# Three projections of the matrix memories moved into the gated recurrence's loop

## The reference

```
hg_q, hg_i, hg_g, hg_f_fwd, hg_f_bwd, ml_q, ml_k, ml_v, ml_o, ml_gates = split(h_all @ w_in)
# first half: gated recurrence, 4 heads of 128, in both directions
log_f = log(lb + (1 - lb) * sigmoid(f_pre)); k_in = (1 - lb) * sigmoid(-f_pre)
hg_o = both_directions(S_t = diag(f_t) S_{t-1} + k_t v_t^T ; o_t = S_t^T q_t)
hg_out = head_rmsnorm(hg_o, hg_norm_w) * silu(hg_g)
# second half: matrix memories, 4 heads, in both directions
qk = silu(short_conv([ml_q, ml_k], conv_w, conv_b))  # 3x3 over the 8 x 64 latent grid, 3 taps over the context
ml_h = both_directions(mlstm(q, k, ml_v, i_gate, log_sigmoid(f_gate)))
ml_out = sigmoid(ml_o) * head_rmsnorm(ml_h, ml_norm_w)
lat_out = concat(hg_out, ml_out)[latent] @ w_out
```

## Time and profile before

| | |
|---|---|
| median of 3 runs | 3689.83 us (3689.51 to 3694.19) |
| the profiled execution | 3686.75 us |
| its span | 3683.8 us |
| PE busy | 3358.1 us, 91% of the span |
| DVE busy | 1669.8 us, 45% |
| ACT busy | 1164.0 us, 32% |
| POOL busy | 976.3 us, 27% |
| mean granted TensorE clock | 0.938 |

### The profile page before, as it was taken

One profiled execution on the slowest core, in us unless ns is written; L12 is line 12 of the kernel. 1 busy time (PEld: TensorE's weight loads), 2 busy tenths in 40 slices (PEclk: granted clock), 3 DMA queues, 4 the chain that ended last, 5 costly groups with the idle time before them and its releaser, 6 DMA issues. The chain is left out here.

```text
span 3683.8 us, 42189 instructions
## 1 busy us (share of the span) xinstructions
PE 3358.1 (91%) x17058; PEld 2672.1 (73%) x17058; DVE 1669.8 (45%) x2625; ACT 1164.0 (32%) x1874; POOL 976.3 (27%) x414
## 2 busy tenths in 40 slices
PE   4999989989999799999997777979999888889998
PEld 3887767867888688888786665358887664568887
DVE  5995576554331323345401886532211576631211
ACT  2232364334442421121322113433222324543322
POOL 0001312433444122323332002024444221024443
PEclk8999999989999899999999778979999888899999
DMA  4232324442233122334321001012233110013332
GB/s 177 93 100 89 134 89 158 154 160 69 98 95 95 65 87 94 126 133 139 107 69 40 1 2 51 1 57 91 96 110 96 46 52 26 1 58 96 96 94 86
DMA packets 91197, 315.98 MB, mean 86 GB/s; under 512 B 10742, under 2 KB 12534, under 8 KB 90234
## 3 DMA queue, kind: packets, MB, share of 16 engines
q1 hardware_dynamic: 88060, 303.69, 25.2%
q10 hardware_dynamic: 2944, 9.60, 0.7%
HBM read 311.16 MB, written 2.10 MB: 85 GB/s over the span
## 5 line engine op out<-in xcount | busy, mean ns | idle before, releaser
L245 POOL TENSOR_TENSOR terms<-streams,terms 128x1024 fp32r<-128x1024 f32 (+2 forms) x410 | 976.1, 2381 | 2685.0 <-ACT terms L233 2685.0
L455 PE MATMUL bank<-terms,terms 128*128 128x512 f32 (+2 forms) x4016 | 1508.7, 376 | 46.8 <-DVE terms L699 17.3
L456 PE MATMUL bank<-terms,terms 128*128 128x512 f32 (+2 forms) x4016 | 1499.7, 373 | 0.0
L457 PE MATMUL bank<-terms,terms 128*128 128x512 f32 (+2 forms) x4016 | 1497.5, 373 | 0.0
L233 ACT ACTIVATE terms<-streams 128x1024 fp32r<-128x1024 f32 (+1 forms) x462 | 475.9, 1030 | 1831.7 <-PE bank L457 1653.6
L455 PEld LDWEIGHTS bank<-terms,terms 128*128 128x128 f32 x4016 | 764.9, 190 | 202.1 <-issue 48.7
L457 PEld LDWEIGHTS bank<-terms,terms 128*128 128x128 f32 x4016 | 765.4, 191 | 132.1
L456 PEld LDWEIGHTS bank<-terms,terms 128*128 128x128 f32 x4016 | 766.4, 191 | 126.1
L1620 DVE TENSOR_TENSOR stage<-stage,bank 128x256 f32<-128x256 f32 (+1 forms) x88 | 54.7, 622 | 596.4 <-ACT stage L1610 596.4
L1063 DVE SCALAR_TENSOR_TENSOR arena<-arena,vec 128x512 f32<-128x512 f32 x240 | 162.4, 744 | 0.2
L1603 DVE TENSOR_TENSOR terms<-stage,terms 128x512 fp32r<-128x512 f32 (+1 forms) x66 | 116.5, 1769 | 0.0
(11 more groups left out here) (320 smaller groups left out, 2984.8 us busy)
## 6 DMA issues: line engine op xcount, KB each, us to landing
streams<-in_ffn_w SPq DMA_DIRECT2D x104, 512.0 KB, 3.5
streams<-in_w_mod SPq DMA_DIRECT2D x72, 512.0 KB, 3.5
streams<-in_w_up SPq DMA_DIRECT2D x44, 512.0 KB, 3.5
streams<-in_w_gu SPq DMA_DIRECT2D x44, 512.0 KB, 3.5
streams<-in_w_ada SPq DMA_DIRECT2D x32, 512.0 KB, 3.5
streams<-in_w_down SPq DMA_DIRECT2D x32, 512.0 KB, 3.5
streams<-in_w_v SPq DMA_DIRECT2D x24, 512.0 KB, 3.8
streams<-in_ffn_w SPq DMA_DIRECT2D x24, 384.0 KB, 3.3
```

The lines of the kernel that those rows point to most:

```text
L245: gp.tensor_tensor(self.low(m), self.raw(n), self.high(m), ALU.subtract).then_inc(self.low_made.sem, 1)
L455: pe.matmul(out, high[:, at], x_high, start=kk == start, stop=False)
L456: pe.matmul(out, high[:, at], x_low, start=False, stop=False)
L457: mm = pe.matmul(out, low[:, at], x_high, start=False, stop=kk == kts - 1)
```

## The change

`MemoryInputs` takes the projections of keys, queries and output gates out of `memory_inputs` and gives one of their eight tiles to each of the recurrence's eight units, in the order keys, queries, output gates. Behind the scores of each level stands one k tile (three matmuls; for the keys two k tiles of one of the two token ranges, the context behind levels 0 to 3 and the latent behind 4 to 7). All use bank 3, and the scores turn through banks 0 to 2. SP fetches and GpSimd makes a low half in each unit; ScalarE evicts the tile and casts a high half after placing the last level's scores. The low halves beside `w_mo` are no longer VectorE's. The stage behind keeps head norms, gates, taps and the gate chain. Taps read unpadded tiles: a tap works on the part of the grid for which its neighbour exists, the centre tap comes first, and each tap waits for the one before it. The gate chain's scans stand behind the taps on VectorE.

```diff
+    dense("w_mk")
+    dense("w_mq")
+    dense("w_mo")
     dense("w_gates")
-    dense("w_mq")
-    dense("w_mk")
-    dense("w_mo")
...
-    k.vector_lows.update(range(k.plan["w_mo"][0][0][0], k.plan["w_out2"][0][0][0]))
...
+    def some(self, pe, n, c, a, b, told=None):
...
+        if a == 0:
+            if uses:
+                pe.wait_ge(k.bank_free[bank].sem, uses)
+            pe.wait_ge(k.low_made.sem, m + 1)
...
+        for kk in range(a, b):
+            at = slice(kk * cols, (kk + 1) * cols)
+            x_high, x_low = self.src(kk, c)
+            pe.matmul(out, high[:, at], x_high, start=kk == 0, stop=False)
+            pe.matmul(out, high[:, at], x_low, start=False, stop=False)
+            mm = pe.matmul(out, low[:, at], x_high, start=False, stop=kk == kts - 1)
...
+    def bank(n, lev):
+        return B[(8 * n + lev) % 3]
...
+        @block.sync
+        def _(sp):
+            for n in range(len(units)):
+                inputs.fetch(sp, n)
+
+        @block.gpsimd
+        def _(gp):
+            for n in range(len(units)):
+                inputs.low(gp, n)
...
             for n in range(len(units)):
+                inputs.keep_context(act, n, tiled)
                 if n + 1 < len(units):
...
                 place(n, levels - 1)
                 place(n, levels)
+                inputs.keep(act, n)
                 act.wait_ge(*turned(n + 1))
...
-                    if lev >= 4:
-                        pe.wait_ge(*merged(6 * n + lev - 3))
-                    elif n and lev < 2:
-                        pe.wait_ge(*merged(6 * n + lev - 1))
+                    if lev >= 3:
+                        pe.wait_ge(*merged(6 * n + lev - 2))
+                    elif n and lev:
+                        pe.wait_ge(*placed(2 * n + lev - 2))
                     elif n:
-                        pe.wait_ge(*placed(2 * n + lev - 3))
+                        pe.wait_ge(*merged(6 * n))
...
                     mm.then_inc(scored.sem, 1)
+                    inputs.multiply(pe, n, lev, tiled)
...
+    def multiply(self, pe, n, lev, tiled):
+        d, i = self.tiles[n]
+        if d is not self.of_keys:
+            d.some(pe, i, 0, lev, lev + 1)
+        else:
+            d.some(pe, i, lev // 4, 2 * (lev % 4), 2 * (lev % 4) + 2, tiled)
...
+    def keep(self, act, n):
+        d, i = self.tiles[n]
+        d.done(act, i)
+        if d is self.of_gates:
+            act.activation(self.k.a(ML_O, 4, 512)[:, i, :], d.bank(i), ACT.Sigmoid).then_inc(*d.free(i))
+        elif d is self.of_queries:
+            act.activation(self.plain(i), d.bank(i), ACT.Copy).then_inc(*d.free(i))
+        else:
+            act.activation(self.plain(2 + i), d.bank(i, 1), ACT.Copy).then_inc(*d.free(i, 1))
+        d.scalar_step(act, i)
...
+    def tap(self, eng, n):
...
+        t, j = divmod(n, 9) if n < 18 else (2 + (n - 18) // 12, (n - 18) % 12)
+        if n:
+            eng.wait_ge(*self.tapped(n))
+        if j < 9:
+            tap = (4, 0, 1, 2, 3, 5, 6, 7, 8)[j]
...
+            r, c = slice(max(0, -dy), 8 - max(0, dy)), slice(max(0, -dx), 64 - max(0, dx))
+            y, x = y[:, r, c], x[:, r.start + dy:r.stop + dy, c.start + dx:c.stop + dx]
...
     def vector(self, dve):
-        k, n = self.k, self.heads.heads
         self.heads.gated(dve)
-        dve.wait_ge(*k.dve_done(n))
-        dve.memset(k.arena[:, ML_QP:ML_Q], 0.0).then_inc(k.more[3].sem, 1)
         self.gates.vector(dve)
+        self.inputs.there(dve)
+        self.inputs.taps(dve, 0, 12)
         self.heads.inverses(dve)
-        self.queries.vector_step(dve, 0)
+        self.inputs.taps(dve, 12, 24)
         self.heads.scaling(dve)
-        self.queries.vector_step(dve, 1)
+        self.inputs.taps(dve, 24, 42)
+        self.chain.forward(dve)
+        self.chain.backward(dve)
```

More of the change, by code:

```diff
@@ L458, in tensor_step @@
                 mm.then_inc(k.piece_done.sem, 1)
+    def some(self, pe, n, c, a, b, told=None):
+        k, cols = self.k, self.cols
+        m, _, kts = self.tiles[n][0]
+        bank, uses = self.banks[n][c]
+        if a == 0:
+            if uses:
+                pe.wait_ge(k.bank_free[bank].sem, uses)
+            pe.wait_ge(k.low_made.sem, m + 1)
+        high, low, out = k.high(m), k.low(m), self.bank(n, c)
+        for kk in range(a, b):
[4 more added lines that the diff above has]
+            mm = pe.matmul(out, low[:, at], x_high, start=False, stop=kk == kts - 1)
+        if b == kts:
+            if c == len(self.chunks) - 1:
+                mm.then_inc(k.piece_done.sem, 1)
+            else:
+                mm.then_inc(told.sem, 1)
     def scalar(self, act):
@@ L1807, in stage_hgrn @@
     B = k.bank
+    tiled = k.more[11]
     units = [(h, d) for h in range(HEADS2) for d in range(2)]
@@ new lines, in forward @@
+    def forward(self, dve):
+        ones, soft, scanned = self.ones, self.soft, self.scanned
+        dve.memset(ones[0:4], 1.0).then_inc(self.folded.sem, 1)
+        dve.wait_ge(*self.smoothed(3))
+        forgets = self.raw[0:4, 1:4:2, :]
+        dve.scalar_tensor_tensor(forgets, forgets, 0.0, soft[0:4], ALU.min, ALU.subtract).then_inc(self.folded.sem, 1)
+        dve.wait_ge(*self.folded(2))
+        g, f, b, m = self.raw[0:4, 0, :], self.raw[0:4, 1, :], self.sums[0:4, 0, :], self.top[0:4, 0, :]
+        dve.tensor_tensor_scan(b, ones[0:4], f, 0.0, ALU.mult, ALU.add).then_inc(scanned.sem, 1)
+        dve.wait_ge(*scanned(1))
+        dve.tensor_tensor(g, g, b, ALU.subtract).then_inc(scanned.sem, 1)
+        dve.wait_ge(*scanned(2))
+        dve.tensor_tensor_scan(m, g, g, -3.0e38, ALU.max, ALU.max).then_inc(scanned.sem, 1)
@@ L2107, in log_forgets, with backward @@
+    def backward(self, dve):
+        ones, sums, top, scanned = self.ones, self.sums, self.top, self.scanned
+        g, f, b, m = self.raw[0:4, 2, :], self.raw[0:4, 3, :], sums[0:4, 1, :], top[0:4, 1, :]
         ctx, lat = slice(CTX - 1, None, -1), slice(TOK - 1, CTX - 1, -1)
@@ L2172, in memory_inputs, with stage_mlstm @@
[L2172 to L2180 removed]
+def stage_mlstm(k, inputs):
+    mq, mk = inputs.queries, inputs.keys
     raw, bound, top = gate_rows(k)
@@ L2496, in block_two @@
     run(k, passes)
-    stage_hgrn(k)
-    run(k, memory_inputs(k, lat_src, src))
-    stage_mlstm(k)
+    inputs = MemoryInputs(k, lat_src, src)
+    stage_hgrn(k, inputs)
+    chain = GateChain(k)
+    gates = Dense(k, "w_gates", src, BOTH, 1, chain.kept)
+    norms = HeadNorms(k, k.a(B2_OUT, HEADS2, 512), "hg_norm", k.a(B2_QG + 4 * 512, HEADS2, 512), HEADS2)
+    run(k, [MemoryStart(k, gates, norms, chain, inputs)])
+    stage_mlstm(k, inputs)
     outs = [k.a(at, 4, 512)[:, h, :] for at in (B2_OUT, ML_OUT) for h in range(HEADS2)]
```

204 lines of the change are left out of this document (94 added, 110 removed).

## The result

| | before | after |
|---|---|---|
| median | 3690.28 us (4 runs) | 3662.30 us (3660.68 to 3671.62, 4 runs) |
| profiled execution | 3686.75 us | 3671.62 us |
| its span | 3683.8 us | 3668.6 us |
| mean granted clock | 0.938 | 0.943 |

The ratio is 0.9928, with a 95% interval of 0.9916 to 0.9941. The forecast was 3665.8 us in a range of 3648 to 3684. The profiled execution of the changed kernel is the slowest of its four; a second set of six gave a median of 3663.07 (ratio 0.9922, 0.9907 to 0.9936).

A forecast was written before the change was run, and what follows sets the result against it. VectorE was taken to set the pace of the recurrence, with TensorE having room while its clock is high. Recurrence +8.0 and stage -31.9 gave -23.9 us, from a median of 3689.83 to 3665.8 us, range 3648 to 3684.

The forecast's parts named there:

- The stage: Memory inputs behind the recurrence: without most projections, VectorE's list sets the length, 54.8 us for 86.7, saving 31.9 us.
- GpSimd's blocking: Unit borders of the recurrence: GpSimd's low halves block VectorE seven times at 2.0 us, +14 us, bounds 0 and 17.
- part 3: GpSimd enters the recurrence: +14 us of blocking on VectorE, while 8.0 us of waits for key-value products go.
- The waits at the carry: VectorE's waits for key-value products at unit borders vanish because the blocking comes first: -8.0 us, bounds 0 and -8.
- Unit 0: First unit of the recurrence: TensorE starts cold and its second level comes 1.6 us late, +1.6 us.
- The key tiles' 2.52 us levels: Units 0 and 1, levels 4 to 7: TensorE's 2.52 us is 0.2 over VectorE's pace; the two units cost 0.4 us.
- Clock dips: Recurrence levels: k tiles at TensorE's low clock exceed VectorE's pace, with few short dips; +2 us, bounds 0 and +20.
- the tail: Behind unit 7: busier TensorE speeds transposes, key-value products and sums; -2 us, bounds -3.5 and +1.
- Rival C: Recurrence: TensorE becomes the bound at the low clock; total +20 us, 3710 us, chance 0.05.
- rival A: Recurrence: GpSimd and VectorE hardly meet, or clock stays high; +14 falls to about +2, total -36, 3654 us, chance 0.17.
- B: Recurrence and stage: clock dips and late ScalarE copies, +12 us, stage 4 us longer; total -9, 3681 us, chance 0.15.
- D: Stage behind the recurrence: dependent taps at 0.9 us, twice blocked, make it 65 us; total -14, 3676 us, chance 0.13.

The follow-up runs named there:

- the taps in turn: Changed kernel with its 42 taps going over the four latent tiles, then the two context tiles, in turn: 3659.15 us, ratio 0.9907 to before.
- small low halves: Changed kernel with GpSimd's eight low halves beside the recurrence cut to 8 of 1024 columns (part of the arithmetic wrong): 3649.12 us, ratio 0.9889 to before.
- the memset: Changed kernel with an unused 2.5 us VectorE memset ahead of the gate chain, to start the memories later: 3659.47 us, ratio 0.9915 to before.
- the low halves on VectorE: Changed kernel with seven of the eight low halves made by VectorE ahead of the carry instead of by GpSimd: 3662.64 us, ratio 0.9924 to before.

## Why the prediction was right, point by point

The direction, the place and the size are right: -24 us forecast, -27 to -28 measured. That the totals lie so close is in part luck: the recurrence came out 4.7 us better than its sum, and the memories and what follows them moved by some us either way from profile to profile, which had no term. By its steps:

- **The stage, -31.9 us forecast, -33.1 measured** (86.9 to 53.8, where I had 54.8). It is VectorE's list, as said. Taps: from 2218.17 to 2254.05, less the reciprocals and scalings between them, 29.7 us with a blocked stretch of about 1.3, so 28.4 for 28.2 forecast. The gate chain took 14.5 for 14.8, the start 3.1 for 3.2. The blocking by GpSimd was 1.3, not 2.1 us: the row of six taps at 2229.80 below, 5.57 us where their shapes (441 to 504 columns) make about 4.3. That this list sets the stage's length is shown by two runs: with the taps in turn both were 4.1 us shorter, and with the memset both were 4.0 longer (2.5 for the memset, 0.8 for a longer blocking, 0.7 in gaps).

```profile
2218.75 3.67 DVE L2136 SCALAR_TENSOR_TENSOR sq<-arena,vec,sq 128x441 f32<-128x441 f32 x5
...
2229.80 5.57 DVE L2136 SCALAR_TENSOR_TENSOR stage<-arena,vec,stage 128x441 f32<-128x441 f32 x6
```

- **GpSimd's blocking, +14 us forecast, 13.4 measured**: seven times 1.91, read from the rows. The place was missed. I had the low half fall on VectorE's first instructions of a unit; it waited beside them and fell on the first product. The Trainium skill (SBUF — State Buffer, Who interferes with whom) has instructions with two inputs in SBUF on the list of those that contend, as the product here. It exempts instructions with at most one such input only outside their modes that use two ports, a condition that the prediction left out. Here GpSimd lost its 1.1 us beside a memset and a tensor_scalar; which mode that one ran in, no run shows. The rows that the price of 2.0 to 2.1 us came from are read almost rightly: part 3 took the two tensor_scalars at 0.3 us, and alone they take 0.41, so that collision cost 2.0 us each. But the price is not what removing the blocking gives back: about 9 us, by the run with small low halves.
- **The waits at the carry, -8.0 us forecast**: all seven borders are free of it, but not mainly for the reason given. I had the blocking cover them. Without the blocking, in the run with small low halves, 2.3 us of wait came back in four places (0.90, 0.70, 0.46, 0.21), not 8.0. The other 5.7 are gone also without it: the granted clock of that recurrence is 0.94, and where it was high at a border (the first three) there is no wait. The blocking does cover a wait where the clock is lower: with most k tiles left out, at 0.82, no border has one.
- **Unit 0, +1.6 forecast**: the first two unit starts lie 21.1 us apart for 20.1, +1.0. **The key tiles' 2.52 us levels, +0.4**: nothing to be seen; unit 1 takes 24.64 us, no more than the others.
- **Clock dips, +2 forecast**: behind unit 0's start two short ones (2134.9 to 2138.3 and 2158.8 to 2162.2 us), and no unit longer for them. This is the term that I had too high, with the tail: **-2 forecast, -3.5 measured** (the last unit with the tail took 33.4 us for 34.9, with a blocking of 1.9 in it). The bound of -3.5 stood in the text and I took less. Both belong to one thing: the clock rose to 0.97, higher than the "over 0.8" that I named.
- **Sum of the recurrence**: +8.0 forecast, +3.3 measured. +1.0 + 13.4 - 8.0 - 3.5 = +2.9, and 0.4 is left unassigned.
- Together -29.8 us from the recurrence's start to that of the memories in the profiles. **What the prediction left out** is that the memories can differ by 7 us from profile to profile. It took "what it took" for granted.

Rival C (TensorE the bound at the low clock) was far off: the clock answered to the added work. Of rival A the first condition (no blocking) is false, by the rows; the second (the clock stays high) is true, but its price of +2 for the low halves is not. B did not come; its sum, +12 and +4 on my -24, is -8 and not -9. D did not come: it had taps at 0.9 us, and they start 0.72 to 0.78 us apart. The dependence is real all the same. It costs 0.12 us a tap against overlap, not 0.035, but the 0.035 is counted from a tap's end, and overlapping taps start 0.08 us ahead of it. The 28.2 us were built from full lengths and were right for that reason.

## What to carry to other kernels

Look for an engine that idles beside the one that sets the pace, and move work of a later stage into its gaps; if that engine is TensorE, the moved matmuls can pay twice, by the clock. Count what comes along with the moved work on the other engines, also where no semaphore ties them: here seven subtractions of GpSimd cost 1.9 us each on VectorE, more than VectorE would have needed for them itself (1.23). Such a cost can hide a wait, so take it out before you call it a gain: here 13.4 us of blocking hid some 2 us of waits and the tail's slower clock, and to be rid of them was worth about 9. Taps on one target cost 0.12 us a step here against steps over several targets in turn.

## What was unexpected of the hardware

- Idleness of TensorE can be dearer than work: the recurrence took 207.5 us at a clock of 0.82 with most of the k tiles left out, and 202.7 at 0.97 with them. About 0.9 of the 4.8 us came from GpSimd's low half falling on another product.
- Engines don't meet only at semaphores: at a border GpSimd and VectorE held each other up, GpSimd losing 1.1 us and VectorE 1.9, with no semaphore between the two instructions.
- One stage of 320 matmuls, with the same 4.6 us of idle time of TensorE, took 99.5, 100.9, 103.8 or 106.9 us, and the same few lengths came back in different kernels, 99.5 and 103.8 in the kernel before too. The Trainium skill (TensorE: Matmul & The Clock Gate, What's actually happening) says that the gate acts on how busy TensorE has been recently. The trace fits that in so far as the late fall came behind waits of 0.60 and 0.91 us; why it then lasted 3.4, 10.2 or 13.7 us, and which of the waits lets the clock fall, was not settled. An edit worth under 5 us ahead of such a stage can be hidden by it, as the low halves on VectorE were.
